# RWKV triangular solve: from 128x128 block products, two heads at a time, to 64x64 products on compact blocks, four heads at a time

## The reference

```python
A_ab = pair(a_dec, b_inv, strict)
A_ak = pair(a_dec, k_inv, strict)
A_rb = pair(r_dec, b_inv, incl)
A_rk = pair(r_dec, k_inv, incl)
rhs = jnp.concatenate([a_dec, jnp.einsum('bhnls,bhnsv->bhnlv', A_ak, v)], axis=-1)
sol = lax.linalg.triangular_solve(jnp.eye(L, dtype=F32) - A_ab, rhs,
                                  left_side=True, lower=True, unit_diagonal=True)
z_state, z_local = sol[..., :N], sol[..., N:]
y_local = jnp.einsum('bhnls,bhnsv->bhnlv', A_rk, v)

def step(S, inp):
    zs, zl, rd, arb, yl, be, ke, vc, sd = inp
    z = jnp.einsum('bhlk,bhvk->bhlv', zs, S) + zl
    y = jnp.einsum('bhlk,bhvk->bhlv', rd, S) + jnp.einsum('bhls,bhsv->bhlv', arb, z) + yl
    S = (S * sd[:, :, None, :] + jnp.einsum('bhlv,bhlk->bhvk', z, be)
         + jnp.einsum('bhlv,bhlk->bhvk', vc, ke))
    return S, y
```

## Time and profile before

| quantity | us |
|---|---|
| median of the timed runs (3467.71 to 3470.72) | 3469.66 |
| span of the profiled execution | 3470.4 |
| from the first product of the solve to the first of the scan (259.93 to 442.54) | 182.6 |
| from there to the first product of the finish (442.54 to 480.27) | 37.7 |

### The profile page before, as it was taken

One profiled execution on the slowest core, in us unless ns is written; L12 is line 12 of the kernel. 1 busy time (PEld: TensorE's weight loads), 2 busy tenths in 40 slices (PEclk: granted clock), 3 DMA queues, 4 the chain that ended last, 5 costly groups with the idle time before them and its releaser, 6 DMA issues.

```text
span 3470.4 us, 42141 instructions
## 1 busy us (share of the span) xinstructions
PE 3248.7 (94%) x15702; PEld 2666.3 (77%) x15702; DVE 2320.3 (67%) x2271; ACT 1580.7 (46%) x1572; POOL 185.6 (5%) x212
## 2 busy tenths in 40 slices
PE   7979979999999979999999997689999999999997
PEld 5869968777888758778787775567888888888885
DVE  4653336567755556467754447568999999999996
ACT  2332213332223334332222224247777777777774
POOL 0000000000000000000000000001111111111111
PEclk9978959999999979999999997689999999999998
DMA  4200003234433203334434210349999999999995
GB/s 178 86 9 1 1 19 112 89 116 145 146 118 105 84 14 113 92 112 149 146 97 133 80 55 25 124 185 404 384 385 378 391 374 391 381 384 386 378 386 209
DMA packets 119396, 638.94 MB, mean 184 GB/s; under 512 B 13480, under 2 KB 13480, under 8 KB 69488
## 3 DMA queue, kind: packets, MB, share of 16 engines
q1 hardware_dynamic: 99168, 561.05, 43.3%
q0 software_dynamic: 20112, 76.24, 7.3%
HBM read 612.59 MB, written 24.64 MB: 184 GB/s over the span
## 4 chain that ended last, share of the span: by engine, by line
PE 85%; DVE 10%; issue 2%; DMA 1%; ACT 1%; DVEq 0%; POOL 0%; SPq 0%; ACTq 0%; POOLq 0%
PE banks L328 30%; PE banks L2901 20%; PE banks L2918 9%; PE banks L1360 7%; PE banks L1866 5%; PE banks L341 3%; DVE chunk_split L301 1%; PE banks L2895 1%; PE banks L760 1%; PE banks L783 1%; PE banks L2886 1%; PE banks L2907 1%; DMA weight_ring<-in_w 1%; PE banks L2257 1%; DVE scratch L1458 0%
## 5 line engine op out<-in xcount | busy, mean ns | idle before, releaser
L328 PE MATMUL banks<-x_scratch,chunk_split 128*128 128x512 f32 x3648 | 850.6, 394 | 36.3 <-DVE x_scratch L315 22.6
L328 PEld LDWEIGHTS banks<-x_scratch,chunk_split 128*128 128x128 f32 x3648 | 687.6, 189 | 191.7 <-issue 48.6
L295 ACT CAST chunk_split<-weight_ring 128x1024 fp32r<-128x1024 f32 x292 | 306.3, 1049 | 962.1 <-PE banks L328 722.5
L2901 PE MATMUL banks<-pair_split,rows 128*128 128x512 f32 x3072 | 710.5, 392 | 2.8 <-DVE pair_split L2656 2.8
L2901 PEld LDWEIGHTS banks<-pair_split,rows 128*128 128x128 f32 x3072 | 578.6, 188 | 130.0 <-DVE pair_split L2656 3.9
L301 DVE TENSOR_TENSOR chunk_split<-weight_ring,chunk_split 128x1024 fp32r<-128x1024 f32 x292 | 356.9, 1222 | 211.0 <-ACT chunk_split L295 202.1
L2918 PE MATMUL banks<-pair_split,hidden_t 128*128 128x512 f32 x1536 | 361.9, 394 | 4.5 <-DVE pair_split L2656 2.8
L2918 PEld LDWEIGHTS banks<-pair_split,hidden_t 128*128 128x128 f32 x1536 | 285.3, 189 | 68.1 <-DVE pair_split L2656 4.4
L2656 DVE TENSOR_TENSOR pair_split<-mixed,pair_split 128x2048 fp32r<-128x2048 f32 x128 | 292.8, 2289 | 34.5 <-ACT pair_split L2651 34.5
L2656 DVE TENSOR_TENSOR pair_split<-scratch,pair_split 128x2048 fp32r<-128x2048 f32 x128 | 290.4, 2288 | 37.5 <-ACT pair_split L2651 37.2
L2656 DVE TENSOR_TENSOR pair_split<-weight_ring,pair_split 128x2048 fp32r<-128x2048 f32 x128 | 290.3, 2288 | 35.7 <-ACT pair_split L2651 35.7
(11 more groups left out here) (628 smaller groups left out, 3857.8 us busy)
## 6 DMA issues: line engine op xcount, KB each, us to landing
weight_ring<-in_weights SPq DMA_DIRECT2D x292, 512.0 KB, 3.6
mixed<-in_w SPq DMA_DIRECT2D x128, 1024.0 KB, 8.4
weight_ring<-in_w SPq DMA_DIRECT2D x128, 1024.0 KB, 8.3
scratch<-in_w SPq DMA_DIRECT2D x128, 1024.0 KB, 9.5
mixed<-in_w_ada POOLq DMA_DIRECT2D x48, 512.0 KB, 3.8
token_sums<-tables POOLq DMA_DIRECT2D x1, 2560.0 KB, 20.9
residual<-in_x POOLq DMA_DIRECT2D x4, 512.0 KB, 10.7
projected<-in_mem POOLq DMA_DIRECT2D x2, 1024.0 KB, 5.2
```

Of the source, the lines that this page charges most:

```text
L295: act.copy(chunk_split[:, 0, at:at + KB * P], flat(ring[:, n % RING])).then_inc(chunk_hi.sem, 1)
L328: mm = pe.matmul(lin.bank(j), chunk_split[:, a, at + k * P:at + (k + 1) * P], lin.split[b][k][:, 0:lin.tokens], start=(k, a, b) == (0, 0, ...
L2901: mm = pe.matmul(banks[:, n, :], rows[:, a, k, :], pair_split[k % SLOTS][:, b, n * T:(n + 1) * T], start=False, stop=(k, a) == (KB - 1, 1))
```

## The change

- The masks are stored as compact halves: two 64-column masks share one 128-column matrix (`HALF_MASKS`), and the constants are one matrix shorter.
- A matrix of one head is now only its 64x64 blocks: 256 words on 128 partitions, the first chunk of a tile on partitions 0 to 63 and the second on 64 to 127. Two matrices share what was one row.
- A product is eight 64x64 `matmul` calls, for each tile one with operands and result of chunk 0 and one of chunk 1.
- A head owns two banks, in quarters of 256 words. Four heads are in flight (`SLOTS`), in two waves; groups are interleaved over the four.
- Group 6 multiplies with the identity in place of the transpose.
- `y_local` is gone from the solve. The masked fifth product moves to groups 5 and 6 and is kept as `ark`; the scan adds `v_tok` times `ark` to the output sums itself, ahead of `arb`. The last step of the scan is a copy.

```diff
-            ON_DVE, ON_ACT = (1, 2, 3, 4, 5, 8, 9, 10), (2, 3, 4, 6, 7, 11)
+            ON_DVE, ON_ACT = (1, 3, 4, 5, 6, 8, 9, 10), (2, 3, 4, 6, 7, 11)
+            SLOTS, GROUPS = 4, 11
-            buf = [{n: spare[7 * q + i] for i, n in enumerate(names)} for q in range(2)]
+            buf = [{n: half_row(spare[(7 * s + i) // 2], 7 * s + i) for i, n in enumerate(names)} for s in range(SLOTS)]
+            def quarter(s, n):
+                return blocks64(banks[:, 2 * s + n // 2, 256 * (n % 2):256 * (n % 2) + 256])
...
                             def mm(out, lhs, rhs):
                                 for tt in range(TT):
-                                    ins = pe.matmul(out(tt), lhs(tt), rhs(tt), start=True, stop=True)
+                                    for c in range(2):
+                                        ins = pe.matmul(out(tt, c), lhs(tt, c), rhs(tt, c), start=True, stop=True)
                                 return ins
 
                             def chan(x):
-                                return lambda tt: x[r, a, tt * P:(tt + 1) * P]
+                                return lambda tt, c: x[r, a, tt * P + 64 * c:tt * P + 64 * c + 64]
 
                             def blk(x):
-                                return lambda tt: tiles(x)[:, tt, :]
+                                return lambda tt, c: x[64 * c:64 * c + 64, tt, :]
+                            def to(n):
+                                return blk(quarter(s, n))
+                            def to_channels(tt, c):
+                                return banks[r, 2 * s + c, tt * 64:tt * 64 + 64]
...
                             elif g == 2:
-                                mm(to_bank(0), chan(k_inv), chan(r_dec))
-                                mm(lambda tt: half[1][:, tt, :], blk(B["AK"]), lambda tt: v_tok[:, tt, hc])
-                                mm(to_bank(2), blk(B["M"]), blk(B["D"]))
-                                ins = mm(to_bank(3), blk(B["D"]), blk(B["M"]))
+                                mm(to(2), blk(B["M"]), blk(B["D"]))
+                                mm(to(3), blk(B["D"]), blk(B["M"]))
+                                ins = mm(to(1), blk(B["AK"]), tok(v_tok))
                             elif g == 3:
-                                mm(lambda tt: bank[0][r, tt, :], lambda tt: v_tok[:, tt, hc], blk(B["D"]))
...
                             elif g == 5:
-                                ins = mm(to_bank(1), blk(B["M2"]), blk(B["X"]))
+                                mm(to(1), blk(B["M2"]), blk(B["X"]))
+                                ins = mm(to(2), chan(k_inv), chan(r_dec))
                             elif g == 6:
-                                for tt in range(TT):
-                                    ins = pe.transpose(bank[2][:, tt, :], tiles(B["X"])[:, tt, :], mat["ident"])
+                                ins = mm(to(0), blk(B["X"]), lambda tt, c: mat["ident"][64 * c:64 * c + 64, 64 * c:64 * c + 64])
...
                     for a, q, r, hc in heads:
-                        mm = pe.matmul(banks[r, a, w], zc[:, q, a, :], RW["arb"][2 * a + q][rows, w], start=c == 0,
+                        pe.matmul(banks[r, a, w], RW["v_tok"][rows, tt, hc], RW["ark"][2 * a + q][rows, tt, :], start=c == 0,
+                                  stop=False, skip_group_check=True)
+                        mm = pe.matmul(banks[r, a, w], zc[:, q, a, :], RW["arb"][2 * a + q][rows, tt, :], start=False,
                                        stop=True, skip_group_check=True)
...
                 dve.wait_ge(pe_step.sem, multiplied(7, 3))
-                dve.tensor_tensor(MIX[:, 4:8, :], RW["y_local"], banks[:, 0:4, :], ALU.add).then_inc(dve_step.sem, 1)
+                dve.tensor_copy(MIX[:, 4:8, :], banks[:, 0:4, :]).then_inc(dve_step.sem, 1)
```

More of the change, by code:

```diff
@@ L74, in constant_matrices, with halves @@
     b16, b64 = (r // 16 == c // 16), (r // 64 == c // 64)
+    def halves(*masks):
+        return np.concatenate([np.concatenate([m[0:64, 0:64], m[64:P, 64:P]], axis=0) for m in masks], axis=1)
     rot = np.zeros((P, P), np.float32)
@@ L1818, in program, with blocks64, half_row @@
         }
+        def blocks64(ap):
+            return ap.rearrange("p (t l) -> p t l", l=64)
+        def half_row(row, n):
+            return blocks64(row[:, 256 * (n % 2):256 * (n % 2) + 256])
         RW.update({
-            "zs": S(4, 4), "z_local": S(8, 4), "y_local": PROJ[:, 21:25, :],
-            "arb": [PROJ[:, 17 + h, :] for h in range(4)] + [S(12 + h)[:, 0, :] for h in range(4)],
+            "zs": S(4, 4), "z_local": S(8, 4),
+            "arb": [half_row(PROJ[:, 17 + h // 2, :], h) for h in range(8)],
+            "ark": [half_row(S(12 + h // 2)[:, 0, :], h) for h in range(8)],
         })
@@ L1936, in act, with mask @@
                             ins.then_inc(act_step.sem, 1)
             def dve(dve):
-                def each(m):
-                    return mat[m].unsqueeze(1).to_broadcast([P, TT, P])
-                for a in range(4):
+                def mask(name):
+                    matrix, half = HALF_MASKS[name]
+                    return mat[matrix][:, 64 * half:64 * half + 64].unsqueeze(1).to_broadcast([P, TT, 64])
+                for wave in range(2):
                     for g in ON_DVE:
-                        for q in range(2):
-                            B, h = buf[q], 2 * a + q
-                            bk = [tiles(banks[:, 4 * q + n, :]) for n in range(4)]
-                            dve.wait_ge(pe_step.sem, multiplied(g, a, q))
+                        for s in range(SLOTS):
+                            B = buf[s]
+                            dve.wait_ge(pe_step.sem, multiplied(g, wave, s))
@@ L1954, in dve @@
-                                ins = dve.tensor_tensor(tiles(B["X"]), tiles(B["M"]), each("ident"), ALU.add)
-                            elif g == 2:
-                                ins = dve.tensor_tensor(tiles(B["D"]), bk[0], each("i64u"), ALU.mult)
+                                link["dve"](dve.tensor_tensor(B["M"], quarter(s, 0), mask("s16u"), ALU.mult))
+                                dve.tensor_tensor(B["ET"], quarter(s, 0), mask("off16u"), ALU.mult)
+                                dve.tensor_tensor(B["D"], quarter(s, 1), mask("s16l"), ALU.mult)
```

121 lines of the change are left out of this document (62 added, 59 removed).

## The result

The changed kernel takes 3369.05 us (median of 4 runs, 3365.95 to 3377.11) against 3469.3 us for the kernel before beside it (the table ahead of the prediction has 3469.66; the median of the same four runs is 3469.3). The ratio is 0.9732, 95% interval 0.9711 to 0.9753. The time is close to that of the first rival (3377 us).

A forecast was written before the change was run, and what follows sets the result against it. The prediction took PE's rate of passes to bound the solve. Solve -36.2, scan +8.1 and start -0.2 summed to -28.3 us, giving a median of 3441.3 us, range 3418 to 3458.

The forecast's parts named there:

- the first rival: Solve: the clock rises to full, 78 us of passes, 83 us in all; total 3377 us; chance 0.07.
- Which clock?: Solve: half clock throughout, as in the scan; 2688 passes at 54 ns, 145.2 us.
- 64-partition products did not raise it: Start of the old solve: such products left the clock at 0.50; used to support half clock.
- The counts: Solve: 168 calls a head (before 84), eight heads, 1344 calls, 2688 passes.
- The price of a pass: PE, 64x64 passes by spacing of starts: 54 ns at half clock, 29 ns at full.
- The rival's 83 us: Solve at full clock: 78 us of passes, some 4 us of waits for DVE, 1.2 us at the end.
- The scan: Eight more `ark` calls per chunk, not hidden: 6.0 us in chunks 1 to 7, 2.1 in chunk 0, together +8.1 us.
- the term of chunk 0: First chunk of the scan: 1.78 us at full clock becomes 3.9 with 64 passes at 54 ns, 2.1 us more.
- ACT's copy of `zs`: End of solve: 512-word copy (0.58) becomes 256 words (0.37), so 0.9 us to the scan's start where it was 1.1.
- The constants: Start: they shrink from 1088 to 1024 KB; at most 0.9 us saved, 0.2 taken.
- No pairing: Solve: pairs on one half of the partitions run one after the other, 110 ns a pass; +107.5 us, 3549 us; chance 0.07.
- The full clock: Same as the first rival: solve at full clock in 83 us, total 3377 us; chance 0.07.

The follow-up runs named there:

- e2_pause: Changed kernel with ACT's copy of k_end done six times more before the solve, so PE stands idle longer there; 3380.96 us, ratio 0.9771.
- e8_group1_twice: e2_pause with the products of group 1 issued twice for the four heads of the first wave; 3409.18 us.
- e5_fill: Changed kernel with twelve 128x128 passes of constants filling PE's pause between solve and scan; 3365.20 us, ratio 0.971.
- e7_two_heads: Changed kernel with two heads in flight in place of four (`SLOTS` 2, four waves); 3376.02 us, ratio 0.973.
- e3_pause_before: Kernel before the change with the same six extra ACT copies ahead of its solve as in e2_pause; 3473.02 us.
- e10_four_quarters: e2_pause with group 1 of each pair of heads interleaved call by call, so neighbouring products lie in four quarters of the array; 3390.83 us.
- e4_no_ark: Changed kernel with the product of `v_tok` with `ark` left out of the scan; 3361.51 us, ratio 0.9699.
- e6_unpaired: Changed kernel with a product's two loops swapped: the four tiles of chunk 0 first, then those of chunk 1; 3380.71 us, ratio 0.9753.
- e11_four_and_fill: Changed kernel with PE's pauses ahead of solve and scan filled by products of constants, and group 1 in four quarters; 3362.91 us, ratio 0.9698.

## Why the prediction was wrong

**The step that failed is "Which clock?"** I took the level of the scan for the level of the shape: same 64x64 products, same pairing, PE busy 95%, clock 0.50. The runs show in its place:
- The scan's products fix no level. In all profiles the scan met 1.00; in six of the eleven with the pause as it is the clock fell about 2 us later and did not come back, in the other five the same products ran at 1.00 to the end. What decides between the two is not shown.
- The changed solve, whose passes follow one another nearly without a gap, kept 1.00 where it met it (79.4 to 79.9 us in three profiles of the changed kernel). Where it met 0.50 the clock rose 3.4 to 5.0 us after group 2 began (e2_pause, e8_group1_twice, e5_fill, e7_two_heads), and then stayed. Even then the solve took 86.7 and 87.1 us and not 146.

That one factor is nearly the whole miss: 2688 passes at 29 ns and not 54, and the solve at 79.9 us and not 146.4, which is 66.5 us of the 72 between forecast and result; 4 us more lie ahead of the solve and 1.5 in the scan. An execution that meets 0.50 at the start of the solve loses 7 us by it, not 66. The row that should have weighed more was my own for the rival: 1.70 us of such products at 1.00, directly behind a gap-free solve. "64-partition products did not raise it" was right for group 1, and e8_group1_twice confirms it; I extended it to groups that read both halves.

**What was right.** The counts: 2688 passes, PE the bound, DVE and ACT kept up. (A head had 88 calls before, four of them transposes of one record each, and not 84; nothing in the sum hangs on it.) The waits in the solve after, longest first, name PE as the one waited for throughout:

```profile
ACT scratch L1946 <- PE banks L1885: 16.4, 2, 8.7
ACT scratch L1959 <- PE banks L1885: 14.1, 3, 6.9
DVE scratch L1982 <- PE banks L1885: 13.0, 12, 3.9
```

The price of a pass at each level: 29 ns at full in the solve; at half 53 ns within a head of e2_pause (48 records in 2.83 us) and 49 ns over the whole of its group 1 (12.5 us for 256 passes), as the passes of two heads overlap where the head changes. The rival's 83 us for the solve at full clock stood 3 us too high: DVE's six operations took 0.33 to 0.46 us each from start to start and not 0.42 throughout, and the other heads covered them. The scan: +8.1 forecast, +6.6 measured; the term of chunk 0 (2.1 us) was too large by the 1.5 us, since the clock falls only 1.9 us into the scan (2.41 us from 335.48 to 337.89, against 1.78).

**Wrong in size.** ACT's copy of `zs` still takes 0.58 us: it takes up 64 partitions and 512 words as before, only in another order, so 1.1 us pass from ACT's start to the scan's first product, as before, where I had 0.9. The constants landed in 13.2 us where they took 15.1, and PE's first product came 1.9 us earlier (21.98 for 23.86); I had 0.2. But e3_pause_before, with the larger constants, had 13.9 us and 22.64, within what the changed kernel's runs show (13.0 to 14.0 us, 21.81 to 22.74), so little or nothing of the 1.9 us is shown to be the change's. The other 2.4 us ahead of the solve lie in the preparation, where the clock changes several times; no run tells what of them is the change's.

**The rivals.** No pairing (0.07) did not happen. The Trainium skill's restriction that row tiles cannot access one PSUM bank at once ("TensorEngine Tiling (Array Packing)", Restrictions and Gotchas) does not hold here for pairs that write different halves of a bank's partitions: 29 ns a pass through the solve shows them side by side. The full clock (0.07) is what came, 8 us below that rival's 3377. It had been the forecast by the rule of the Trainium skill's clock gate page ("TensorE: Matmul & The Clock Gate", Part 1), that sustained activity releases the throttle. The solve of the changed kernel agrees with that rule; group 1 doesn't, which kept PE busy for 25.9 us in e8_group1_twice without raising the clock.

**Still open.** Why group 1 does not raise the clock is narrowed down, not settled: it differs from group 2 in reading one half of the partitions and in its shape of pairs, and e10_four_quarters changed both. Why the clock falls in one scan and not in the next is open too. And which level an execution meets at the solve and at the scan varies from one to the next with the same code: in the profiles of e5_fill and e7_two_heads the solve began at 0.50, in five others without the pause at 1.00 (the changed kernel's three, e4_no_ark and e6_unpaired). That was not controlled, and it explains only a part of the changed kernel's spread (3357 to 3379 us): the rest of the program, behind the scan's last sum, differs by 5.5 us among its three profiles, and the kernel before spreads as widely.

## What to carry to other kernels

When a stage's clock is to be forecast, don't take it from a neighbour with the same instructions: ask which level the stage meets, which of its products raised or lost it in the trace, and whether the neighbour always runs at the level that the one trace shows; and price the stage at both levels with a real chance for each. Small block-diagonal fp32 products were far better issued as products of quarters here (79.9 us for 182.6), in an order in which neighbours lie in different quarters (without that order the solve took 18 us more). A chain of small products with pauses may run at either level: here the lower one costs 14 us, and spare products of constants in the pause ahead of it brought no gain clear of noise.

## What the runs showed of the hardware that I had not expected

- Four quarters at once: at the low level 64x64 fp32 passes came every 27 ns with four quarters in turn (e10_four_quarters), every 53 ns with two (e2_pause); at the full level every 15 ns (e11_four_and_fill) and 29 ns, but with pauses of 1 to 2 us between stretches of the former.
- PE looks past its next instructions: with eight passes in a row in one quarter it still took 36.5 ns a pass and not 58 (e6_unpaired).
- The same products can run at either level of the clock: the same scan took 28.3 us or 42.0 us, as it kept the 1.00 that it met or lost it at its start.
- Not every stream without a gap raises the clock: 25.9 us of products that read one half of the partitions left it at 0.50 (e8_group1_twice).
